# Token norms in quarters: sums by four column tiles, root and reciprocal on packed rows, spread by small products, and one pass for the norms of queries and keys

## The chip, the cores and the metric

The kernel runs on one core of a Trainium2 chip as one program. The metric is the device time of one execution, in microseconds, as a median over runs. Beside it stands a profile of one more execution.

## What is computed

Two transformer blocks of two layers each run on 512 tokens of width 1024; the first block also has 256 context tokens. All of it is float32. What bears on the change are the norms over the features of each token:

```python
def rmsnorm(x, g):
    y = x * lax.rsqrt(jnp.mean(x * x, axis=-1, keepdims=True) + RMS_EPS)
    return y * g
def modulate(x, g, shift, scale):
    return rmsnorm(x, g) * (1 + scale) + shift
def layer_norm(x, g, b):
    mu = jnp.mean(x, -1, keepdims=True)
    var = jnp.mean(jnp.square(x - mu), -1, keepdims=True)
    return (x - mu) * lax.rsqrt(var + LN_EPS) * g + b
```

- `modulate` stands before the mixer and before the mixture of experts in both layers of the first block: 768 tokens (256 context and 512 latent) three times, 512 tokens once. A last `rmsnorm` ends the block.
- In the first mixer `rmsnorm` is also taken of the query latent (384 features, 3 chunks of 128), of the key-value latent (256 features, 2 chunks), and of each head of 64 features in `gq` (8 heads, 4 chunks) and `gk` (2 heads, 1 chunk), for 768 tokens.
- `layer_norm` stands four times in the second block, for 512 tokens.
- The vectors for shift and scale come from `silu(c) @ w_ada`, a matrix of 2 x 1024 x 6144 that is read once.

## The kernel before

Activations lie with features on the 128 partitions (8 chunks of 128) and tokens along the free axis. The program is a row of stages. Each is a block with one instruction list for each engine, and all engines meet between two stages. Loads that a stage names as `ahead` or `beside` are issued by SyncE at that stage's start.

**A norm stage** (`norm_stage`) takes a list of jobs, one for each span of tokens (256 or 512). In a job ScalarE squares each chunk (L507). TensorE multiplies it with a matrix of ones, which leaves the sum over all features in all 128 rows for each token (L533). ScalarE takes the root (L511), VectorE the reciprocal (L547) and then one multiply for each chunk by gain and reciprocal (L552), and ScalarE adds the shift (L516). A layer norm (`center=True`) first sums the features themselves (L527) and subtracts the mean (L545). A float32 product shows as two matmul records. ScalarE loads another function table at the first root of a stage in which the table is not in place.

**Which stages there are:** `mod0` (2 jobs), `norm_qk`, `ffn0` (2), `mod1` (2), `ffn1` (1), `final` (1, no shift), and the layer norms `ln00`, `ln01`, `ln10`, `ln11` (1 each). `norm_qk` has 14 jobs: for either span of tokens one for the query latent, one for the key-value latent, one for each chunk of `gq`, one for `gk`; its root and total are held in two buffers each.

**The conditioning** (class `Conditioning`) is `w_ada` in 48 units of 1 MB, 8 units to a group, 6 groups. A unit is multiplied by `multiply` (L388): four matmuls with 32 columns of weights each, which write to four quarters of the partitions and read four different pieces of 512 columns. A finished group is copied by ScalarE (L395), turned by TensorE (L402) and added to the bias by VectorE (L410). This work goes beside other stages: a `Beside(ada, fetched, units, done)` says which units SyncE fetches in the stage, which units TensorE multiplies after which step, and which group is finished after which step. From unit 16 on five slots of memory go round, so unit u is fetched when unit u-5 has been multiplied. Units 8 to 15 are beside `mod0`, 16 to 29 beside `norm_qk`, 30 to 39 beside `ab_up`, 40 to 47 beside `rope`.

**The first mixer** is `ab_in` (projections), `norm_qk`, `ab_up` (38 products with the up-projections, copied out by ScalarE and VectorE in turn), `rope` (14 items; for each a matmul that swaps pairs (L917) and three VectorE operations; TensorE is at most two items ahead; then two small matmuls of `Distances`, their copies, and 8 copies by ScalarE (L948)), and attention.

## Time and profile before

| | us |
|---|---|
| median of 3 runs | 4196.33 (4196.19 to 4197.29) |
| profiled execution | 4192.28, its span 4190.4 |
| TensorE busy in the span | 3682.4 (88%) |
| VectorE busy | 2510.7 (60%) |
| ScalarE busy | 1570.1 (37%) |
| GpSimd busy | 194.9 (5%) |
| DMA, mean over the span | 161 GB/s |

The span runs from the first to the last instruction. The shares are means over stages with different limits: what a change in a stage is worth has to be read from that stage's own rows.

### The profile page before, as it was taken

To read this page: it belongs to the slowest core of one execution; us is meant where nothing else is said; L and a number is where in the kernel's file an instruction comes from. 1 tells how busy PE (TensorE), PEld (TensorE's weight loads), DVE (VectorE), ACT (ScalarE), POOL (GpSimd) and SP (SyncE) were. 2 spreads that over 40 slices of the span, in tenths; PEclk is the share of its full clock that TensorE was granted. 3 is DMA by queue.
4 is the path that set the end of the run, shared out by engine and by line. 5 is a ranking of instruction groups with operands and counts; after the bars stand their busy time and mean duration, and the time that the engine had idled before them with its cause. 6 is when DMAs were issued, how large, how long until landed. Compare 5 with 4: busy or idle time off the path is not lost. (4 is left out here: it accounts for less than half of the span.)

```text
span 4190.4 us, 51613 instructions
## 1 busy us (share of the span) xinstructions
PE 3682.4 (88%) x18221; PEld 2836.7 (68%) x18221; DVE 2510.7 (60%) x3105; ACT 1570.1 (37%) x2030; POOL 194.9 (5%) x306
## 2 busy tenths in 40 slices
PE   7988998599999589877799998698899979879997
PEld 4523766588888379555688886485687858557875
DVE  2044663588888442764688886545555566356654
ACT  2012652377777310462577786113111021111101
POOL 0000000111111100000111111000000000000000
PEclk9988998699999699998899999799999989989999
DMA  7064811699999220002899995421233246113321
GB/s 251 33 229 125 222 28 46 246 361 383 377 367 355 84 81 22 21 1 98 297 361 362 367 362 201 131 71 46 70 96 94 80 61 91 31 40 97 94 92 49
DMA packets 372842, 672.85 MB, mean 161 GB/s; under 512 B 48238, under 2 KB 246715, under 8 KB 366560
## 3 DMA queue, kind: packets, MB, share of 16 engines
q1 hardware_dynamic: 350477, 639.24, 45.6%
q0 software_dynamic: 21600, 31.51, 2.1%
q8 instruction: 89, 1.46, 0.1%
q14 instruction: 49, 0.40, 0.0%
q10 hardware_dynamic: 627, 0.24, 0.0%
HBM read 651.46 MB, written 66.58 MB: 171 GB/s over the span
## 5 line engine op out<-in xcount | busy, mean ns | idle before, releaser
L1844 DVE TENSOR_TENSOR moe0b_w_lo<-moe_raw,moe0b_w_hi 128x2048 fp32r<-128x2048 f32 x118 | 264.5, 2287 | 57.5 <-ACT moe0b_w_hi L1766 54.1
L1844 DVE TENSOR_TENSOR moe1b_w_lo<-moe_raw,moe1b_w_hi 128x2048 fp32r<-128x2048 f32 x112 | 251.1, 2288 | 55.0 <-ACT moe1b_w_hi L1766 51.8
L1766 ACT ACTIVATE moe0b_w_hi<-moe_raw 128x2048 fp32r<-128x2048 f32 x118 | 218.9, 1922 | 31.5 <-PEq L1373 31.5
L1766 ACT ACTIVATE moe1b_w_hi<-moe_raw 128x2048 fp32r<-128x2048 f32 x112 | 207.9, 1925 | 23.6 <-PEq L1373 23.6
L507 ACT ACTIVATE ln_squares<-all_x 128x512 f32<-128x512 f32 x32 | 19.2, 630 | 388.8 <-DVE all_x L545 388.8
L1700 PE MATMUL moe0b_gate_ps<-moe0b_w_hi,moe0b_feats_hi 128*128 128x512 f32 x264 | 110.7, 419 | 10.0 <-DVE moe0b_feats_lo L1850 5.9
L1700 PE MATMUL moe1b_gate_ps<-moe1b_w_hi,moe1b_feats_hi 128*128 128x512 f32 x256 | 107.2, 419 | 10.0 <-DVE moe1b_feats_lo L1850 5.9
L1844 DVE TENSOR_TENSOR moe0b_w_lo<-all_h,moe0b_w_hi 128x2048 fp32r<-128x2048 f32 x48 | 107.2, 2286 | 1.8 <-PE moe0b_up_ps L1700 1.8
L1844 DVE TENSOR_TENSOR moe1b_w_lo<-all_h,moe1b_w_hi 128x2048 fp32r<-128x2048 f32 x48 | 107.2, 2284 | 1.7 <-PE moe1b_up_ps L1700 1.7
L1700 PE MATMUL moe0b_up_ps<-moe0b_w_hi,moe0b_feats_hi 128*128 128x512 f32 x264 | 104.3, 395 | 0.0
L1700 PE MATMUL moe0b_gate_ps<-moe0b_w_lo,moe0b_feats_hi 128*128 128x512 f32 x264 | 104.3, 395 | 0.0
L1700 PE MATMUL moe0b_up_ps<-moe0b_w_lo,moe0b_feats_hi 128*128 128x512 f32 x264 | 104.2, 395 | 0.0
L1700 PE MATMUL moe0b_up_ps<-moe0b_w_hi,moe0b_feats_lo 128*128 128x512 f32 x264 | 103.9, 394 | 0.0
L1700 PE MATMUL moe0b_gate_ps<-moe0b_w_hi,moe0b_feats_lo 128*128 128x512 f32 x264 | 103.8, 393 | 0.0
L1700 PE MATMUL moe1b_up_ps<-moe1b_w_lo,moe1b_feats_hi 128*128 128x512 f32 x256 | 101.0, 394 | 0.0
L1700 PE MATMUL moe1b_up_ps<-moe1b_w_hi,moe1b_feats_hi 128*128 128x512 f32 x256 | 100.9, 394 | 0.0
L1700 PE MATMUL moe1b_gate_ps<-moe1b_w_lo,moe1b_feats_hi 128*128 128x512 f32 x256 | 100.8, 394 | 0.0
L1700 PE MATMUL moe1b_gate_ps<-moe1b_w_hi,moe1b_feats_lo 128*128 128x512 f32 x256 | 100.6, 393 | 0.0
L1700 PE MATMUL moe1b_up_ps<-moe1b_w_hi,moe1b_feats_lo 128*128 128x512 f32 x256 | 100.6, 393 | 0.0
L2834 ACT ACTIVATE ffn1u_mixed<-ffn1u_mixed 128x512 f32<-128x512 f32 x22 | 13.9, 632 | 214.9 <-DVE ffn1u_mixed L2794 214.9
L2834 ACT ACTIVATE ffn0u_mixed<-ffn0u_mixed 128x512 f32<-128x512 f32 x22 | 13.9, 632 | 214.9 <-DVE ffn0u_mixed L2794 214.9
L1109 DVE TENSOR_REDUCE attn_top<-attn_scores 128x1 f32<-128x768 f32 (+1 forms) x96 | 72.3, 776 | 36.8 <-PE attn_scores L1026 36.8
(640 smaller groups left out, 10442.8 us busy)
## 6 DMA issues: line engine op xcount, KB each, us to landing
moe_raw<-in_moe_w_gate SPq DMA_DIRECT2D x166, 512.0 KB, 5.8
moe_raw<-in_moe_w_up SPq DMA_DIRECT2D x166, 512.0 KB, 10.4
all_h<-in_moe_w_down SPq DMA_DIRECT2D x128, 512.0 KB, 8.0
moe_raw<-in_moe_w_down SPq DMA_DIRECT2D x128, 512.0 KB, 9.6
all_ahead<-in_ffn_w_up SPq DMA_DIRECT2D x88, 512.0 KB, 5.0
all_ahead<-in_moe_w_gate SPq DMA_DIRECT2D x62, 512.0 KB, 6.0
all_ahead<-in_moe_w_up SPq DMA_DIRECT2D x62, 512.0 KB, 11.0
y_rows<-all_zero SPq DMA_DIRECT2D x43, 512.0 KB, 6.7
```

The costliest lines, as they stand in the source:

```text
L507: nc.scalar.activation(squares[n % n_sq][:, c, 0:j.n], j.dst[c] if center else src, ACT.Square).then_inc(squared, 1)
L1109: V.tensor_reduce(top[:, s:s + 1], scores[s][:, 0:t.keys], AX.X, ALU.max, negate=True).then_inc(topped, 1)
L1700: last = nc.tensor.matmul(acc[:], x[:, c, :], w[:, m, j, :], start=c == 0 and step == 0, stop=c == DC - 1 and step == 2)
L1766: A_.activation(w_hi[r % HIGH][:], raw[slot][:], ACT.Copy).then_inc(rounded, 1)
L1844: V.tensor_tensor(w_lo[r % SPLIT][:], raw[r % RAW][:], w_hi[r % HIGH][:].bitcast(F32), ALU.subtract).then_inc(split, 1)
L2834: nc.scalar.activation(mixed[s][:], mixed[s][:], ACT.Silu).then_inc(silu_ready, 1)
```

## The change

- **Sums.** A chunk of n tokens is no longer summed by one matmul with 128 columns of ones over all n tokens, but by four with 32 columns each, every one over a quarter of the tokens (`QuadRows.add`). Quarter q lands in partitions 32q to 32q+31, so the total of 512 tokens has 128 columns in place of 512.
- **Root and reciprocal** are taken once for a stage, on these packed rows: 128 columns for 512 tokens, 192 for 768.
- **Spread.** Four small products with a constant matrix `pick` (64 rows each, two quarters of the tokens in either half of the rows) bring the reciprocals back to all partitions and all tokens (`QuadRows.spread`); VectorE reads them from PSUM. A layer norm does the same with the mean, which is scaled on packed rows first.
- **Squares.** Where nothing is centred, VectorE squares chunks 1, 4 and 7 and ScalarE the other five. With two jobs all squares come first, then one root and one reciprocal, then all scaling. The work beside a stage comes at its end.
- **`norm_qk`** becomes `latent_norm_stage`: 10 parts of 768 tokens, squared by ScalarE and VectorE in turn through a ring of three buffers, all sums in one PSUM tile (seven kinds of sum, each in its own row of a quarter), one root, one reciprocal, then seven spreads through two buffers. It loads two constants first (`norm_sums`, 112 KB, and `norm_pick`, 896 KB), on which the first sum waits.
- **Units** of the conditioning: 2 beside `norm_qk` (16 and 17, at its end), 19 beside `ab_up` (18 to 36), 11 beside `rope` (37 to 47). Groups 2 and 3 are finished in `ab_up`, 4 and 5 in `rope`.
- The constant `half_ones` (64 KB) gives way to `pick` (128 KB) in the first stage, and `rope` puts the table `by_bucket` into memory of `wkv`.

```diff
+    sums, pick = np.zeros((PART, NORM_KINDS, QUAD), np.float32), np.zeros((PART, NORM_KINDS, 2, PART), np.float32)
+    for q in range(QUADS):
+        for c in range(NORM_CQ):
+            for half in range(2):
+                rows = slice(half * HEAD, (half + 1) * HEAD)
+                sums[rows, c, 2 * c + half], pick[q * QUAD + 2 * c + half, c, q % 2, rows] = 1.0 / HEAD, 1.0
+        for kind, size in ((NORM_CQ, Q_LORA), (NORM_CKV, KV_LORA)):
+            sums[:, kind, NORM_CQ + kind], pick[q * QUAD + NORM_CQ + kind, kind, q % 2, :] = 1.0 / size, 1.0
+    k["norm_sums"], k["norm_pick"] = sums, pick
...
+class QuadRows:
+
+
+
+
+    def __init__(self, nc, n):
+        self.nc, self.m = nc, n // QUADS
+
+    def add(self, out, columns, x, start, stop):
+        for q in range(QUADS):
+            last = self.nc.tensor.matmul(out[q * QUAD:(q + 1) * QUAD, :], columns, x[:, q * self.m:(q + 1) * self.m], start=start, stop=stop)
+        return last
+
+    def spread(self, out, pick, rows, into):
+        for h in range(2):
+            group = slice(h * PAIR, (h + 1) * PAIR)
+            for i in range(2):
+                last = self.nc.tensor.matmul(out[:, h, i * self.m:(i + 1) * self.m], pick[group, i, :], rows[group, :], start=True, stop=True)
+            last.then_inc(into, 1)
+
+
+def halves(x):
+    return x.rearrange("p (h m) -> p h m", h=2)
+
...
+            act.wait_ge(summed, 1)
+            nc.scalar.activation(root[:], total[:, 0:n_tok // QUADS], ACT.Sqrt, scale=inv_n, bias=P.eps[:, eps:eps + 1]).then_inc(rooted, 1)
+            for n, j in enumerate(jobs):
                 if j.bias is not None:
...
+            if center:
+                for n, j in enumerate(jobs):
+                    for c, src in enumerate(j.src):
+                        last = quads[n].add(mean[:, cols[n]], P.ones[:, 0:QUAD], src, c == 0, c == C - 1)
+                last.then_inc(mean_ready, 1)
+                pe.wait_ge(mean_taken, 1)
+                for n in steps:
+                    quads[n].spread(mean_by_half[n], P.pick, mean_rows[:, cols[n]], mean_out)
...
+                    last = quads[n].add(total[:, cols[n]], P.ones[:, 0:QUAD], squares[n][:, c, :], c == 0, c == C - 1)
+            last.then_inc(summed, 1)
+            pe.wait_ge(inverted, 1)
+            for n in steps:
+                quads[n].spread(by_half[n], P.pick, root[:, cols[n]], root_spread)
+            if beside is not None:
+                for n in steps:
                     beside.tensor(pe, n)
...
+            V = nc.vector
+            if center:
+                dve.wait_ge(mean_ready, 1)
+                V.tensor_scalar(mean_rows[:], mean[:, 0:n_tok // QUADS], -inv_n, None, ALU.mult).then_inc(mean_taken, 1)
+                dve.wait_ge(mean_out, 2 * len(jobs))
+                for n, j in enumerate(jobs):
+                    for c, src in enumerate(j.src):
+                        V.tensor_tensor(halves(j.dst[c]), halves(src), mean_by_half[n], ALU.add).then_inc(centered, 1)
...
+                    if on_dve[c]:
+                        V.tensor_tensor(squares[n][:, c, :], src, src, ALU.mult).then_inc(by_dve, 1)
+            dve.wait_ge(rooted, 1)
+            V.reciprocal(root[:], root[:]).then_inc(inverted, 1)
+            if center:
+                dve.wait_ge(by_act, n_act * len(jobs))
+            dve.wait_ge(root_spread, 2 * len(jobs))
+            for n, j in enumerate(jobs):
+                for c, src in enumerate(j.src):
+                    V.scalar_tensor_tensor(halves(j.dst[c]), halves(j.dst[c] if center else src), j.gain[c], by_half[n],
+                                           ALU.mult, ALU.mult).then_inc(scaled, 1)
+            if beside is not None:
+                for n in steps:
                     beside.vector(dve, n)
...
+def latent_norm_stage(nc, P, K, tag, parts, eps, ahead, beside):
...
+        def _(sp):
+            sp.dma_start(sums[:], K["norm_sums"]).then_inc(consts_in, 16)
+            sp.dma_start(pick[:], K["norm_pick"]).then_inc(consts_in, 16)
+            ahead.start(sp)
+            beside.sync(sp)
+
+        @block.scalar
+        def _(act):
+            for n in range(0, len(parts), 2):
+                if n >= RING:
+                    act.wait_ge(added, n - RING + 1)
+                nc.scalar.activation(squares[n % RING][:], parts[n][1], ACT.Square).then_inc(by_act, 1)
+            act.wait_ge(added, len(parts))
+            nc.scalar.activation(root[:], total[:, 0:m], ACT.Sqrt, bias=P.eps[:, eps:eps + 1]).then_inc(rooted, 1)
+            for n in range(len(order)):
+                beside.scalar(act, n)
+
+        @block.tensor
+        def _(pe):
+            pe.wait_ge(consts_in, 32)
+            for n, (kind, _, _) in enumerate(parts):
+                pe.wait_ge(by_dve if n % 2 else by_act, n // 2 + 1)
+                quads.add(total[:, 0:m], sums[:, kind, :], squares[n % RING], n == 0, n == len(parts) - 1).then_inc(added, 1)
+            pe.wait_ge(inverted, 1)
+            for n, kind in enumerate(order):
+                if n >= 2:
+                    pe.wait_ge(scaled, ends[n - 2] + 1)
+                quads.spread(spread[n % 2], pick[:, kind], root, spread_ready)
+                beside.tensor(pe, n)
+
+        @block.vector
+        def _(dve):
+            V = nc.vector
+            for n in range(1, len(parts), 2):
+                if n >= RING:
+                    dve.wait_ge(added, n - RING + 1)
+                V.tensor_tensor(squares[n % RING][:], parts[n][1], parts[n][1], ALU.mult).then_inc(by_dve, 1)
+            dve.wait_ge(rooted, 1)
+            V.reciprocal(root[:], root[:]).then_inc(inverted, 1)
+            dve.wait_ge(added, len(parts))
+            for n, kind in enumerate(order):
+                dve.wait_ge(spread_ready, 2 * (n + 1))
+                for _, x, gain in [part for part in parts if part[0] == kind]:
+                    V.scalar_tensor_tensor(halves(x), halves(x), gain, spread[n % 2][:, :, 0:2 * m], ALU.mult, ALU.mult).then_inc(scaled, 1)
+                beside.vector(dve, n)
...
-                       beside=Beside(ada, range(16, 35), {n: (16 + n,) for n in range(14)}, {10: (2,)}))
+            parts = [(NORM_CQ, cq[:, c, :], col("mla_q_norm")(c)) for c in range(QC)]
+            parts += [(NORM_CKV, ckv[:, c, :], col("mla_kv_norm")(c)) for c in range(KVC)]
+            parts += [(c, gq[:, c, :], P.gq_gain[:]) for c in range(H_B // 2)]
+            parts += [(NORM_GK, gk[:], col("gqa_k_norm")(0))]
+            latent_norm_stage(nc, P, K, "norm_qk", parts, 0, up_weights,
+                              Beside(ada, range(16, 21), {6: (16, 17)}, {}))
...
-                              beside=Beside(ada, range(35, 40), {3 * n + 1: (30 + n,) for n in range(10)}, {12: (3,), 32: (4,)}))
-
+                              beside=Beside(ada, range(21, 42), {2 * n: (18 + n,) for n in range(19)}, {12: (2,), 28: (3,)}))
+
+            distances.by_bucket = wkv[0:T5_BUCKETS + 1].rearrange("p c n -> p (c n)")[:, 0:distances.SPAN]
...
-                       Beside(ada, range(40, 48), {n + 4: (40 + n,) for n in range(8)}, {13: (5,)}), distances)
+                       Beside(ada, range(42, 48), {n + 3: (37 + n,) for n in range(11)}, {6: (4,), 13: (5,)}), distances)
```

## Rows read from the trace of the kernel before

**Rows 1.** Windows by stage: `mod0`, `norm_qk`, `ab_up`, `rope`, `ffn0`, `mod1`, `ffn1`, `final`, `ln00`.
```profile
core 0: us, PE busy (x) PEld busy (x) DVE busy (x) ACT busy (x) POOL busy (x), PEclk, DMA share, GB/s
37.40:72.10 34.70, 23.24 (x101) 10.62 (x101) 13.94 (x19) 18.28 (x36) 0.00 (x0) 0.80 0.75 302
199.50:262.10 62.60, 35.86 (x157) 10.08 (x157) 46.77 (x36) 16.95 (x35) 0.00 (x0) 0.82 0.91 354
262.10:342.80 80.70, 77.55 (x272) 31.18 (x272) 13.58 (x22) 8.81 (x21) 0.00 (x0) 0.97 0.19 65
342.80:387.30 44.50, 29.40 (x100) 6.64 (x100) 27.80 (x44) 7.29 (x11) 0.00 (x0) 0.76 0.59 217
684.60:715.50 30.90, 13.13 (x32) 6.79 (x32) 13.75 (x18) 17.82 (x35) 0.00 (x0) 0.75 0.00 0
1444.60:1477.60 33.00, 15.20 (x32) 8.59 (x32) 13.75 (x19) 17.84 (x36) 0.00 (x0) 0.71 0.20 64
1946.00:1964.40 18.40, 7.14 (x17) 3.00 (x17) 8.74 (x9) 11.57 (x18) 0.00 (x0) 0.78 0.00 0
2647.60:2667.40 19.80, 9.24 (x16) 3.75 (x16) 8.74 (x9) 6.25 (x11) 0.00 (x0) 0.76 0.33 106
2969.60:2995.80 26.20, 14.21 (x32) 5.85 (x32) 13.62 (x17) 12.14 (x18) 0.00 (x0) 0.90 0.31 80
```

**Rows 2.** Timeline of `ffn0`: start, us, engine, line, operation, shapes, count, idle before.
```profile
684.62 2.56 ACT L507 ACTIVATE ffn_squares<-all_x 128x256 f32<-128x256 f32 x8 [73.44 <-PEq L603]
687.20 1.28 ACT L511 ACT_TABLE_LOAD   x1
688.85 0.47 ACT L511 ACTIVATE ffn_root<-ffn_total,all_eps 128x256 f32<-128x256 f32 x1 [0.37 <-PE ffn_total L533]
689.36 1.75 DVE L547 RECIPROCAL ffn_root<-ffn_root 128x256 f32<-128x256 f32 x1 [5.03 <-ACT ffn_root L511]
691.14 3.26 DVE L552 SCALAR_TENSOR_TENSOR all_h<-all_x,all_scale,ffn_root 128x256 f32<-128x256 f32 x8
694.87 4.25 ACT L507 ACTIVATE ffn_squares<-all_x 128x512 f32<-128x512 f32 x8
695.54 9.41 PE L533 MATMUL ffn_total<-ffn_squares,all_ones 128*128 128x512 f32 x16 [6.72 <-ACT ffn_squares L507]
704.98 0.69 ACT L511 ACTIVATE ffn_root<-ffn_total,all_eps 128x512 f32<-128x512 f32 x1 [5.86 <-PE ffn_total L533]
705.70 3.35 DVE L547 RECIPROCAL ffn_root<-ffn_root 128x512 f32<-128x512 f32 x1 [11.30 <-ACT ffn_root L511]
709.09 5.39 DVE L552 SCALAR_TENSOR_TENSOR all_h<-all_x,all_scale,ffn_root 128x512 f32<-128x512 f32 x8
709.88 5.36 ACT L516 ACTIVATE all_h<-all_h,all_mod 128x512 f32<-128x512 f32 x8 [4.21 <-DVE all_h L552]
```

**Rows 3.** Timeline of `ln00`: the sum for the mean, and the centring.
```profile
2969.57 7.11 PE L527 MATMUL ln_mean<-all_x,all_ones 128*128 128x512 f32 x16 [1.05 <-PEq L603]
2976.72 4.87 DVE L545 SCALAR_TENSOR_TENSOR all_x<-ln_mean,all_x 128x512 f32<-128x512 f32 x8 [7.46 <-PE ln_mean L527]
```

**Rows 4.** Timeline of TensorE beside `mod0`: eight units of the conditioning.
```profile
59.54 7.16 PE L388 MATMUL early_ada_acc<-early_ring,all_cond 128*32 128x512 f32 x64
```

**Rows 5.** Groups by shape, TensorE: busy us, mean ns of one, idle before.
```profile
L1050 PE MATMUL attn_n_mixed<-attn_n_probs_t,all_h 128*64 128x128 f32 x768 | 48.8, 277 | 0.0
L1026 PE MATMUL attn_n_scores<-na_k,na_q 64*128 64x256 f32 x128 | 20.4, 377 | 0.0
```

**Rows 6.** Timeline of weight loads in `mod0`: the last unit there.
```profile
65.63 0.16 PEld L388 LDWEIGHTS early_ada_acc<-early_ring,all_cond 128*32 128x32 f32 x8 [0.78 <-DMA early_ring<-in_w_ada]
```

**Rows 7.** DMA issues in `norm_qk`: KB each, median us to landing.
```profile
ab_up_wq<-in_mla_w_q_up SPq DMA_DIRECT2D x1, 1152.0 KB, 6.0
```

**Rows 8.** Timeline of `ab_up`: one unit of the conditioning between two products.
```profile
303.90 1.06 PE L388 MATMUL ab_up_ada_acc<-all_ahead,all_cond 128*32 128x512 f32 x8
```

**Rows 9.** Timeline of ScalarE at the end of `rope`.
```profile
380.74 5.96 ACT L948 ACTIVATE l_ka<-low_kr 32x768 f32<-32x768 f32 x8 [0.39 <-DVE l_gk L934]
```

More of the change, by code:

```diff
@@ L488, in norm_stage @@
         block = ctx.enter_context(nc.Block())
-        first = np.cumsum([0] + [len(j.src) for j in jobs]).tolist()
+        steps = range(len(jobs))
+        on_dve = [not center and c % 3 == 1 for c in range(C)]
+        n_act, n_dve = on_dve.count(False), on_dve.count(True)
+        inv_n = jobs[0].inv_n
         if ahead is not None or beside is not None:
@@ new lines, in _ @@
+            if beside is not None:
+                for n in steps:
+                    beside.vector(dve, n)
+def latent_norm_stage(nc, P, K, tag, parts, eps, ahead, beside):
+    n_tok, RING = TOK, 3
+    m = n_tok // QUADS
+    with ExitStack() as ctx:
+        sb, ps, sem = scope(nc, ctx, tag)
+        quads = QuadRows(nc, n_tok)
+        sums, pick = sb("sums", [PART, NORM_KINDS, QUAD]), sb("pick", [PART, NORM_KINDS, 2, PART])
+        squares = [sb(f"squares{n}", [PART, n_tok]) for n in range(RING)]
+        root = sb("root", [PART, m])
+        total = ps("total", [PART, BANK])
+        spread = [ps(f"spread{n}", [PART, 2, BANK]) for n in range(2)]
+        consts_in, by_act, by_dve, added = sem("consts_in"), sem("by_act"), sem("by_dve"), sem("added")
+        rooted, inverted, spread_ready, scaled = sem("rooted"), sem("inverted"), sem("spread_ready"), sem("scaled")
+        block = ctx.enter_context(nc.Block())
+        order = [kind for n, (kind, _, _) in enumerate(parts) if n == 0 or parts[n - 1][0] != kind]
+        ends = [max(n for n, part in enumerate(parts) if part[0] == kind) for kind in order]
+        @block.sync
+        def _(sp):
[40 more added lines that the diff above has]
+                beside.vector(dve, n)
@@ L569, in modulate_jobs @@
         bias=[P.mod[:, l, 3 * which * DC + c, w:w + 1] for c in range(DC)],
-        sums=P.ones, size=D,
+        size=D,
     ) for t, w in spans]
@@ L2172, in lat_norm_job @@
                             gain=[gain(c) for c in range(DC)], bias=None if bias is None else [bias(c) for c in range(DC)],
[L2173 removed]
+                    size=D)]
 def final_norm(nc, P, ahead):
```

108 lines of the change are left out of this document (41 added, 67 removed).

## The prediction

> **What bounds the kernel now.** I went first to the windows by stage, since the change touches ten stages of very different kinds and their busy shares can't be averaged [rows 1]. The reader is to see that a norm stage is no engine's stage: in `ffn1` 18.4 us hold 7.1 of TensorE, 8.7 of VectorE and 11.6 of ScalarE, one behind the other. `ab_up` is different: TensorE is busy for 77.6 of 80.7 us, so whatever is added to its list there comes on top. `norm_qk` has the DMA engines at 0.91 for 62.6 us at 354 GB/s: its 14 jobs run beside a stream of units, and the two hold each other up.
>
> The timeline of `ffn0` shows the chain inside a norm [rows 2]: squares, sum (its last record ends 5.9 us after the last square), root, reciprocal, scaling with the shift one chunk behind, and then the same again for the second job. Only the first root has a table load before it (1.28), which begins when the squares end (684.62 + 2.56) and lies under the sum. A layer norm has a sum of 7.1 and a centring of 4.87 ahead of that [rows 3].
>
> **The prices.** *Adding a chunk.* 16 records over 512 columns take 7.11, so 0.444 each, and 128 columns would be 0.111 [rows 3]. Do four column tiles run side by side? The 64 records of eight units take 7.16, that is 0.112 each for 512 columns: yes, four at a time [rows 4]. A quarter of that is 0.028 for 128 columns and 0.22 for the 8 records of a chunk. That is the lower bound. The nearest row in size has 128 columns and two tiles side by side: 48.8/768 = 0.0635, which is 0.008 over the half of 0.111 [rows 5]. If the 0.008 is what a record costs besides its columns, a chunk takes 8 x 0.036 = 0.3, which I use. If 0.0635 is a floor for any record, it takes 0.51, the upper bound. With no overlap at all it would be 0.89.
>
> *A spread.* 8 records with full-width weights and 64 rows. Such records of 256 columns take 20.4/128 = 0.159 where one after the other would be 0.222, thus 0.64 to 0.89 for 512 tokens [rows 3, 5]; with the hand-over I take 0.95, and 1.8 at half clock. For two jobs I take 1.6 (1.3 of columns and a second start).
>
> *Packed rows.* The root falls from 0.69 to 0.47 as 512 columns become 256, so 0.37 for 128 and 0.42 for 192; the reciprocal from 3.35 to 1.75, so 0.95 and 1.35 [rows 2]. Scaling is unchanged at 0.41 for 256 columns and 0.67 for 512, with the last shift 0.76 behind [rows 2]. Reading the factor from PSUM is bounded by the centring, which reads PSUM and takes 0.61 a chunk: a possible gain of 0.5 a stage [rows 3].
>
> *The table load.* It costs nothing now because the sum covers it. With the sum gone quickly it stands bare: 1.28 after ScalarE's last square. So the shorter sum doesn't end the wait; the table load is late next.
>
> **Stage by stage.** `ffn0`: ScalarE does five of eight squares, 1.60 + 2.66 = 4.26, and VectorE's three are done sooner; table 1.28; root 0.42; reciprocal 1.35; spread 1.6; scaling 3.26 + 5.39; last shift 0.76; hand-overs and the change of stage 0.6. That is 18.9 where the window has 30.9: 12.0 less [rows 1, 2]. `mod1` works at a lower clock (0.71 in its window), so I add 1.3 to the spread and 0.6 to the sums: 20.8 for 33.0, 12.2 less.
>
> `ffn1`: 2.66 + 1.28 + 0.37 + 0.95 + 0.95 + 5.39 + 0.76 and 0.5 of hand-overs = 12.9 for 18.4: 5.5 less. `final` has no shift, but the lower clock: 2.66 + 1.28 + 0.4 + 0.37 + 0.95 + 1.8 + 5.39 + 0.6 = 13.5 for 19.8: 6.3 less.
>
> `ln00`: mean 8 x 0.3 and a start, 2.5; scaling it on 128 columns 0.3; spread 0.95; centring 4.87, with the squares following; last square 0.6; table 1.28; root 0.37; reciprocal 0.95; spread 0.95; scaling 5.39; shift 0.76; hand-overs 0.7. That is 19.6 for 26.2: 6.6 less, and 26.4 for four, the other three taken alike.
>
> `mod0`: the last unit's data holds its end. TensorE waits for it until 65.63 [rows 6], and the loads before it don't change. After it came the unit, the wait for ScalarE's shifts, copy, turn and bias up to 72.1 [rows 1]. All norm work is now done some 9 us before 65.6 (37.4 + 18.9 = 56.3), so only the wait goes: 2.7 less, not 12.
>
> `norm_qk`: the first sum waits for 1008 KB of constants. SyncE issues them first; the nearest load of that size, 1152 KB, landed 6.0 us after its issue [rows 7], so 205.5. Behind them the weights and the units come 2.5 us later, which hides: only units 16 and 17 are wanted, and at the end. Ten chunks of 768 tokens: 8 x 0.05 = 0.4 at full clock and 0.73 at half; TensorE has idled for 6 us, so 0.6 each, to 211.5. Root, reciprocal and hand-overs 1.9; first spread 1.4, to 214.9. VectorE scales ten parts of 768 columns in 0.94 each; the five kinds with one part are held by spreads of 1.4, 2 us more, so 226.3; the two units end at 227.6. About 28.5 us for 62.6: 34.1 less, with 25.5 (everything at full clock and overlapped) to 35 (spreads at half clock) as bounds.
>
> What it hands on: `ab_up` gets nine more units of 1.06 [rows 8] into an engine that has no room: 9.5 more. Their data is in time (5 MB a loop of ten products, 20 us or more). `rope` gets units 37 to 39, about 0.8 more; group 4's copy and turn between items (0.53 as a 512-column ScalarE operation, 0.44 for four records of 128 columns, and hand-overs) 1.5; unit 41's load in front of its tables, up to 2.5 us of a queue, 1.5; and at the end unit 47 now stands behind the last but one item, so that copy, turn, the `Distances` products (1.1) and their copies come before ScalarE's eight copies, which now start right behind VectorE's last operation [rows 9]: 3.0. Together 6.8. The three stages: 34.1 - 9.5 - 6.8 = 17.8 less.
>
> **The sum.** 12.0 + 12.2 + 5.5 + 6.3 + 26.4 + 2.7 + 17.8 = 82.9. The profiled execution took 4192.28, so 4109.4; the median of the runs is 4.05 above it, so 4113.4. The 64 KB more in the first stage are 0.2 us at 354 GB/s.
>
> **One rule against it.** Records of 128 columns were seen at 0.0635 with two tiles side by side, and nothing in the profile shows four tiles at that size [rows 5]. The Trainium skill (TensorE: Matmul & The Clock Gate, section "Wait — 56ns, not 53.3ns?") says that the engine's sequencer can spend about 62 ns on each matmul, which binds once the array's work for it is shorter. By that rule a chunk takes 0.50, and packing into quarters stops paying at that point; the row is consistent with it as well as with my reading.
>
> **The rivals.**
> - *Each record has a floor of 0.0635.* A chunk costs 0.51. The mean takes 1.7 more in each layer norm (6.7), the sums of `ffn0` and `mod1` 16 x 0.51 = 8.2 and now outlast squares and table load by 2.9 each (5.8). For it: the row is exactly there. Against: half of 0.111 explains most of it. Time: 4126.
> - *The first mixer gives nothing back.* The conditioning work is the same, and `ab_up` has no idle TensorE; if constants, half clock and the longer `rope` take 17.8 together, 4131. For it: the DMA share of 0.91 in `norm_qk`, so the old stage was also useful transfer time [rows 1]. Against: 65 GB/s in `ab_up` leaves room.
> - *The quarters run one after the other.* 0.89 a chunk at full clock: 23 more in the layer norms, 7.6 in the single norms, 11.5 in `ffn0` and `mod1`, 7.4 in `norm_qk`: 4163. Against it stand the 64 records [rows 4].
> - *Slower: one after the other and at half clock,* since TensorE works little in these stages. At 1.78 a chunk the layer norms lose 80, the single norms 22, the double ones 33, `norm_qk` 21, against my sum: 4268. It passes no gain at about 1.2 us a chunk.
> - *No gain in all* would need just that 1.2: 4196.
>
> **How the numbers follow.** My case 0.70, the floor 0.17, the mixer 0.07, serial at full clock 0.03, slower 0.02, no gain 0.01. The predicted time is my case's. Below: sums at 0.22 (2.5), spreads at 0.64 (3.5), the mixer's lower bounds (6), factors from PSUM (4), so 4097. Above: 0.51 a chunk (12.5), all spreads at half clock (9), the mixer's upper bounds (9.5), so 4144. The range 4096 to 4145 holds the floor and the mixer too; about 2 in 10 lies outside. About 0.2%, 8 us, is what a measurement of this kernel can tell from no change: faster 0.97, same 0.01, slower 0.02.
>
> **What would show it.** Adding a chunk: TensorE's records in the layer norms' mean, 64 records in 2.4 us (1.8 or 4.1 by the bounds, 7 or more if serial). The table load bare between the last square and the root, with no TensorE work above it. Reciprocals of 0.95 and 1.35. `norm_qk` about 28 us with TensorE idle for the first 6. `ab_up` near 90, `rope` near 51 with ScalarE's eight copies 3 us behind VectorE's last addition. `mod0` shorter by less than 4. I am wrong if TensorE's clock stays low in the layer norms (spreads of 1.8), if the ring in `norm_qk` starves, or if the next stages begin slower because TensorE has idled more before them.

## The result and the profile after

The changed kernel takes 4099.08 us (median of 4 runs, 4098.90 to 4101.79) where the kernel before takes 4196.81: ratio 0.9768, 95% interval [0.9751, 0.9785], 97.7 us less. Predicted were 4113.4 and a range of 4096 to 4145. The profiled execution took 4101.79; it is compared below with the profiled 4192.28 of before, a difference of 90.5 both in time and in span.

The windows by stage of the changed kernel, in the order of [rows 1] with the first attention between `rope` and `ffn0` (from each stage's first operation to the next stage's):

```profile
core 0: us, PE busy (x) PEld busy (x) DVE busy (x) ACT busy (x) POOL busy (x), PEclk, DMA share, GB/s
38.80:71.90 33.10, 20.88 (x212) 7.85 (x213) 12.94 (x24) 15.15 (x29) 0.00 (x0) 0.65 0.79 318
199.06:225.00 25.94, 15.12 (x153) 8.92 (x153) 15.70 (x16) 4.53 (x6) 0.00 (x0) 0.80 0.84 329
225.00:311.54 86.54, 85.54 (x344) 30.95 (x344) 13.77 (x23) 8.81 (x21) 0.00 (x0) 1.00 0.72 249
311.54:357.84 46.30, 31.99 (x128) 7.07 (x128) 28.25 (x45) 7.90 (x13) 0.00 (x0) 0.78 0.46 176
357.84:582.90 225.06, 209.25 (x1664) 151.23 (x1664) 138.14 (x293) 141.09 (x324) 0.00 (x0) 0.96 0.51 122
660.20:678.50 18.30, 6.34 (x144) 5.14 (x145) 12.74 (x23) 14.56 (x28) 0.00 (x0) 0.64 0.00 1
1407.30:1425.80 18.50, 6.49 (x144) 5.67 (x144) 12.75 (x24) 14.60 (x29) 0.00 (x0) 0.59 0.36 114
1895.30:1908.40 13.10, 4.38 (x72) 2.63 (x72) 8.20 (x12) 9.69 (x15) 0.00 (x0) 0.58 0.01 2
2592.30:2606.10 13.80, 4.37 (x72) 3.49 (x72) 9.74 (x17) 5.90 (x10) 0.00 (x0) 0.62 0.50 159
2908.19:2927.40 19.21, 8.22 (x144) 4.58 (x144) 11.48 (x18) 11.80 (x18) 0.00 (x0) 0.67 0.42 110
```

`norm_qk` fell from 62.6 to 25.9. `ab_up`, whose TensorE now works 85.5 of 86.5 us, grew by 5.8, `rope` by 1.8. Such a change can be booked by the shift of each stage's first operation between the two traces. Summed up, in us saved against what was forecast:

| part | forecast | by the starts |
|---|---|---|
| `mod0` | 2.7 | 0.2 |
| first mixer to the start of its attention | 17.8 | 29.3 |
| that attention and `ab_out` | 0 | -5.1 |
| `ffn0`, `mod1` | 12.0, 12.2 | 12.6, 14.5 |
| `ffn1`, `final` | 5.5, 6.3 | 5.3, 7.5 |
| `ln00`, `ln01`, the other two together | 6.6, 6.6, 13.2 | 7.0, 8.0, 15.0 |
| drifts of the stages between | 0 | -3.8 |
| sum | 82.9 | 90.5 |

A second trace of the changed kernel (under `changed_again` below) gives the norm stages the same to 0.5 us, but only 26.0 for the mixer and 84.0 in all. The norms' column is firm, then, and the mixer's good to some 3 us.

The timeline of `ffn0` after, the answer to [rows 2]:

```profile
660.19 4.24 ACT L556 ACTIVATE ffn_squares<-all_x 128x256 f32<-128x256 f32 x10 [73.23 <-PEq L729]
660.21 2.90 DVE L606 TENSOR_TENSOR ffn_squares<-all_x 128x256 f32<-128x256 f32 x6 [0.32 <-PEq L729]
660.65 5.08 PE L498 MATMUL ffn_total<-ffn_squares,all_ones 128*32 128x64 f32 x128 [1.56 <-ACT ffn_squares L556]
664.45 1.28 ACT L558 ACT_TABLE_LOAD   x1
665.81 0.42 ACT L558 ACTIVATE ffn_root<-ffn_total,all_eps 128x192 f32<-128x192 f32 x1
666.26 1.35 DVE L608 RECIPROCAL ffn_root<-ffn_root 128x192 f32<-128x192 f32 x1 [3.15 <-ACT ffn_root L558]
667.67 1.26 PE L505 MATMUL ffn_spread<-ffn_root,all_pick 64*128 64x64 f32 x16 [1.94 <-DVE ffn_root L608]
668.98 8.49 DVE L614 SCALAR_TENSOR_TENSOR all_h<-all_x,all_scale,ffn_spread 128x256 f32<-128x256 f32 x16 [1.36 <-PE ffn_spread L505]
669.49 8.73 ACT L563 ACTIVATE all_h<-all_h,all_mod 128x256 f32<-128x256 f32 x16 [3.26 <-DVE all_h L614]
```

One chain where there were two, with squares of 4.24, a root of 0.42, a reciprocal of 1.35 and a scaling of 8.49 (forecast: 4.26, 0.42, 1.35 and 8.65). One detail will matter: the sum's last record ends at 660.65 + 5.08 = 665.73, the very moment at which the table load ends.

The mean in `ln00`, the answer to [rows 3]:

```profile
2908.19 1.95 PE L498 MATMUL ln_mean<-all_x,all_ones 128*32 128x128 f32 x64 [1.05 <-PEq L729]
2910.20 0.29 DVE L598 TENSOR_SCALAR ln_mean_rows<-ln_mean 128x128 f32<-128x128 f32 x1 [2.33 <-PE ln_mean L498]
2910.55 0.72 PE L505 MATMUL ln_mean_spread<-ln_mean_rows,all_pick 64*128 64x128 f32 x8 [0.41 <-DVE ln_mean_rows L598]
2911.35 4.87 DVE L602 TENSOR_TENSOR all_x<-all_x,ln_mean_spread 128x512 f32<-128x512 f32 x8 [0.86 <-PE ln_mean_spread L505]
```

64 records in 1.95 are 0.030 each: four column tiles side by side, with 0.24 for a chunk where 0.30 was taken, near the lower bound of 0.22. The records' starts show how: four follow each other 0.006 to 0.007 us apart, and the next four begin 0.109 us after the first of them.

No run below separates the shorter sums from the packed root and reciprocal; only the rows do. In `ln00` the mean's sum is 5.2 shorter and its scaling and spread take back 1.2, and the root went from 0.69 to 0.37 and the reciprocal from 3.35 [rows 2] to 0.95, for which the second spread takes back 1.4.

### The profile page after: what moved, and what is told of

Read it like the earlier page. It is cut to its first block and busy times, and to the rows that moved or that the text cites. A ratio compares the mean times of both kernels' runs of the same rounds, so it can differ in the third digit from the quotient of the medians.

```text
span 4099.9 us, 53555 instructions
## 1 busy us (share of the span) xinstructions
PE 3623.2 (88%) x19213; PEld 2822.3 (69%) x19213; DVE 2468.4 (60%) x3112; ACT 1543.6 (38%) x1975; POOL 194.2 (5%) x306
```

## The experiments

Each was timed beside the kernel before, whose median lay between 4196.4 and 4198.2 throughout; four groups of runs used four chips. The experiments' own runs spread over 5 to 20 us, the longest mostly at a lower mean granted clock. Effects of a few microseconds are therefore read from the traces, by the shifts of the stages' starts. These have a spread too. Between the two traces of the changed kernel, with no edit at all, the starts drift apart by 1.6 us up to `norm_qk`, 3.6 up to the attention and 6.5 up to the end. `norm_qk` took 25.9 in one and 27.0 in the other, `ab_in` 127.2 and 128.5. So a shift counts only where it arises in the stage that was edited and is larger than that stage's own spread.

### The norms alone, and the mixer alone

```diff
 norms_only: nine stages by the new norm_stage
-latent_norm_stage(nc, P, K, "norm_qk", parts, 0, up_weights, Beside(ada, range(16, 21), {6: (16, 17)}, {}))
+old_norm_stage(nc, P, "norm_qk", norm_jobs(...), 0, ahead=up_weights,
+               beside=Beside(ada, range(16, 35), {n: (16 + n,) for n in range(14)}, {10: (2,)}))
 ab_up and rope: the units of before
 mixer_only: the reverse; the nine stages by old_norm_stage
```

> The nine other norm stages as changed, but the stage norm_qk, its two neighbours' share of the conditioning units and the rope's order as before. My theory, by the shift of starts between the two traces: the nine norm stages took 12.6, 14.5, 5.3, 7.5, 7.1, 8.0 and some 15 for the last two, about 70 us, and the first mixer 29, so the time goes back up by some 29 to about 4128. Rival 1 (the mixer gives everything back; the 5.2 us that attention takes longer in the trace of the changed kernel are caused by it): the mixer is worth only 24 and the time is about 4122. Rival 2 (most of the gain is the mixer's, by overlap with other stages that the starts don't show): above 4140.

> The stage norm_qk and the units as changed, all other norm stages as before. My theory: the gain is the mixer's alone, 29 us of 4196.8, so 4168, and with the run of the norms alone the two gains add up to the whole 98 within 2 us. Rival (the slower starts of ab_up, rope and attention eat the shorter norm_qk): 4190 or more. If the gains of both runs add up to much less than 98, the parts help each other, which the stage windows don't show.

Norms alone also loads the constant `half_ones` again, which the old `norm_qk` reads. Measured: 4124.3 (4121.2 to 4130.0, ratio 0.9826 [0.9813, 0.9839]) and 4170.3 (4167.6 to 4175.9, ratio 0.9934 [0.9920, 0.9948]), with 4196.95 before. The norms are worth 72.7 and the mixer 26.7, together 99.3 for the 97.7 of the whole: the parts add up. In the trace of the norms alone, the attention starts 26.9 us later than in the changed kernel's, but `ab_out` only 21.7 later. The attention took 219.9 us there and 225.1 in the changed kernel. So the 5 us there belong to the changed mixer, as the first rival said. The price itself lies between that rival's 24 and the theory's 29: 26.7 with the mixer alone, 25.0 as the whole less the norms.

### All squares on ScalarE

```diff
-        on_dve = [not center and c % 3 == 1 for c in range(C)]
+        on_dve = [False] * C
```

> As changed, but ScalarE makes all squares of the stages without a mean (VectorE made three of eight). It undoes the split and leaves the packing. My theory: ScalarE's squares precede the table load and the root, so ffn0 and mod1 lose 6 squares there (0.37 and 0.53 each, 2.6 us a stage), ffn1 and final 3 (1.6 each), mod0 nothing, as it waits for its units: 8.4 us more, 4107.5. Rival (the sum hides them, so the split is worth nothing): 4099, with the table load then still bare behind the last square.

Measured: 4110.2 (4105.9 to 4115.0, ratio 0.9788 [0.9774, 0.9801]). By the starts `ffn0` lost 2.4, `mod1` 3.1, `ffn1` 1.6 and `final` 1.2: 8.3 where 8.4 was expected, so VectorE's three squares of eight are 8 of the 98 us, and the rival (nothing) falls. The rest of the longer span lies in stages that the edit doesn't touch.

### The root's table ahead of the squares

```diff
-        on_dve = [not center and c % 3 == 1 for c in range(C)]
+        warm = sb("warm", [PART, 1])
+        on_dve = [not center and c % 2 == 1 for c in range(C)]
...
         def _(act):
+            nc.scalar.activation(warm[:], P.eps[:, eps:eps + 1], ACT.Sqrt).then_inc(warmed, 1)
```

> As changed, with a root of one element as ScalarE's first instruction of each norm stage, and four of eight squares on VectorE instead of three. The table load of 1.28 us then comes before the squares instead of between the last square and the root; in a layer norm it lies under the mean. My theory (the load stands bare in each stage): 1.28 less in each of four layer norms, and in the others as much as the squares' new split allows, 1.2 each in ffn0 and mod1 (1.28 + 8 squares of 0.37 to 0.53 beside VectorE's 0.97 a pair) and 0.5 each in ffn1 and final: 8.5 in all, 4090.6. Rival 1 (the sums end after the load anyway, so the load hides): 4099. Rival 2 (a Square needs another table than the root, so each stage then loads twice): 5 to 10 slower, with two table loads in each stage.

Measured: 4099.9 (4096.4 to 4105.2, ratio 0.9768 [0.9755, 0.9782]). In all nothing was gained, as rival 1 said; the theory fell. The timeline of `ffn1`, first of the changed kernel and then of this one:

```profile
1895.98 3.16 PE L498 MATMUL ffn_total<-ffn_squares,all_ones 128*32 128x128 f32 x64 [1.77 <-ACT ffn_squares L556]
1898.03 1.28 ACT L558 ACT_TABLE_LOAD   x1
1899.32 0.37 ACT L558 ACTIVATE ffn_root<-ffn_total,all_eps 128x128 f32<-128x128 f32 x1
```

```profile
1893.44 1.28 ACT L551 ACT_TABLE_LOAD   x1 [45.21 <-PEq L731]
1893.48 2.50 DVE L608 TENSOR_TENSOR ffn_squares<-all_x 128x512 f32<-128x512 f32 x4 [0.32 <-PEq L731]
1895.51 3.59 PE L498 MATMUL ffn_total<-ffn_squares,all_ones 128*32 128x128 f32 x64 [3.14 <-ACT ffn_squares L558]
1899.15 0.37 ACT L560 ACTIVATE ffn_root<-ffn_total,all_eps 128x128 f32<-128x128 f32 x1 [2.13 <-PE ffn_total L498]
```

In the changed kernel the sum ends at 1899.14 and the table load at 1899.31. They run side by side, so taking the load away can win 0.2 there. In the edited kernel the load delays ScalarE's first square, and TensorE, which takes the chunks in order, starts 2.1 us into the stage instead of 0.7 and stands until then: the root begins 5.7 us after the stage's start where it began 4.0 after. A TensorE that takes VectorE's chunks first was not tried, so the edit shows what this order costs and not what the load alone is worth. Only the layer norms, where the load hides under the mean, gained: from the start of the mean to the root 9.48 instead of 10.01 in `ln00`, half a microsecond, and between 0.5 and 1.0 in the other three, where 1.28 was expected. Now the root of `ln00` waits 0.78 for the sum.

### The mean, one column tile after the other

```diff
-                    for c, src in enumerate(j.src):
-                        last = quads[n].add(mean[:, cols[n]], P.ones[:, 0:QUAD], src, c == 0, c == C - 1)
+                    for q in range(QUADS):
+                        for c, src in enumerate(j.src):
+                            last = nc.tensor.matmul(mean[q * QUAD:(q + 1) * QUAD, cols[n]], P.ones[:, 0:QUAD],
+                                                    src[:, q * m:(q + 1) * m], start=c == 0, stop=c == C - 1)
```

> As changed, but the records of the mean in the four layer norms come in another order: the 16 of one column tile together, then the next tile's, instead of one for each of the four tiles in turn. Same records, same columns, same sums. My theory: the 0.030 us that a record of 128 columns takes are four tiles working side by side, and neighbours in the queue must be for different tiles, so now a record takes 0.111 (a quarter of 0.444), the mean 7.1 instead of 1.95, and four layer norms 20.6 more: 4119.6. Rival (the engine works on quarters in any order, or a record is bound by its issue and not by its columns): 1.95 again and 4099.

Measured: 4113.9 (4106.0 to 4122.0, ratio 0.9797 [0.9783, 0.9810]). The mean of `ln00` in that kernel's timeline, and its first 12 records alone:

```profile
2909.98 5.93 PE L575 MATMUL ln_mean<-all_x,all_ones 128*32 128x128 f32 x64 [1.04 <-PEq L732]
2915.94 0.29 DVE L601 TENSOR_SCALAR ln_mean_rows<-ln_mean 128x128 f32<-128x128 f32 x1 [6.29 <-PE ln_mean L575]
2909.98 1.47 PE L575 MATMUL ln_mean<-all_x,all_ones 128*32 128x128 f32 x12 [1.04 <-PEq L732]
```

The same 64 records take 5.93 instead of 1.95, at the full granted clock in both: 0.093 each on average where I expected 0.111. Within one tile the price was right: the 12 records take 1.47, of which the last one's own length is 0.27, so they start 0.109 apart. What is missing to 0.111 arises at the three changes of tile: around each some eight records stand in pairs, 0.005 to 0.030 apart, as records of two tiles side by side would. By the stages' lengths the four layer norms are 16.7 longer (3.4 to 4.6 each; 20.6 expected). So the tiles work side by side when neighbours in the queue are for different tiles, and the mechanism, not the number of records, makes the gain.

### Where `mod0`'s gain went

```diff
             def _(sp):
-                if ahead is not None:
-                    ahead.start(sp)
                 if beside is not None:
                     beside.sync(sp)
+                if ahead is not None:
+                    ahead.start(sp)
```

> As changed, but in mod0 the eight conditioning units are fetched before the 2 MB of ab_in's first weights. My theory (the stage mod0 is held by the last unit's data, 67.7 us in the trace, so nothing of the norm's gain shows): the units land 5 to 6 us sooner and mod0 ends some 3 us sooner, then at its next bound, ab_in's weights, which land at about 67.7 instead: 4096. Rival (ab_in waits for all the later data anyway, so what mod0 gains ab_in loses): ab_in ends as before, 4099.

Measured: 4096.8 (4095.0 to 4106.9, ratio 0.9769 [0.9756, 0.9783]). The timeline of TensorE's weight loads at the end of `mod0`, of the changed kernel and then of this one:

```profile
67.72 0.16 PEld L403 LDWEIGHTS early_ada_acc<-early_ring,all_cond 128*32 128x32 f32 x8 [2.31 <-DMA early_ring<-in_w_ada]
71.88 0.29 PEld L928 LDWEIGHTS ab_in_bank<-all_h,all_ahead 128*128 128x128 f32 x1 [0.92 <-issue]
```

```profile
61.62 0.20 PEld L403 LDWEIGHTS early_ada_acc<-early_ring,all_cond 128*32 128x32 f32 x8 [2.34 <-DMA early_ring<-in_w_ada]
66.91 1.35 PEld L928 LDWEIGHTS ab_in_bank<-all_h,all_ahead 128*128 128x128 f32 x4 [2.32 <-DMA all_ahead<-in_ab_w_in]
```

The last unit comes 6.1 us sooner, `ab_in` starts 5.0 sooner and also ends 4.9 sooner, so the rival falls; now its weights hold it. Of the 5.0, 0.8 was there at `mod0`'s start, and 4.2 are the stage's (28.9 instead of 33.1), more than the 3 expected: the DMA engines' share in `mod0` rose from 0.79 to 0.92.

### ScalarE's copies first in `rope`

```diff
             def _(act):
+                act.wait_ge(rotated, 1)
+                for src, dst in spread:
+                    nc.scalar.activation(dst, src, ACT.Copy).then_inc(copied, 1)
...
-                act.wait_ge(rotated, len(items))
-                for src, dst in spread:
-                    nc.scalar.activation(dst, src, ACT.Copy).then_inc(copied, 1)
```

> As changed, but in the stage rope ScalarE makes its eight copies of the shared key first, as soon as the first item is turned, and the conditioning's rows and the distances after them. My theory (the end of rope is ScalarE's serial list: turn's copy, distances, then 5.95 us of copies that start 2.8 us behind VectorE's last addition): the copies hide under VectorE's work, rope ends with the distances' copies at about 352.5 instead of 357.8, and the time is 5 less: 4094. Rival (the attention behind it is held by something else, its weights or its code, and gives the 5 back): rope is 5 shorter and the time 4099.

Measured: 4091.0 (4082.2 to 4093.7, ratio 0.9739 [0.9726, 0.9753]). In the changed kernel ScalarE's end of `rope`, the answer to [rows 9], was

```profile
350.84 0.74 ACT L2338 ACTIVATE l_distance_rows<-rope_distance_acc 8x512 f32<-8x512 f32 x2 [1.70 <-PE rope_distance_acc L2333]
351.61 5.95 ACT L1074 ACTIVATE l_ka<-low_kr 32x768 f32<-32x768 f32 x8
```

and VectorE's last addition ends at 348.86, so the copies start 2.8 behind it, as forecast. With the copies first, the attention starts 7.9 us sooner, 5.5 of them `rope`'s (2.4 stood there before it began), where `rope` took 39.7 to 41.2 in the nine traces without an edit there and 34.1 here; 1.1 is given back in the attention, whose stall (below) it doesn't touch.

### A constant in two parts in `norm_qk`

```diff
-            pe.wait_ge(consts_in, 32)
+            pe.wait_ge(sums_in, 16)
...
+            pe.wait_ge(pick_in, 16)
             pe.wait_ge(inverted, 1)
```

> As changed, but in norm_qk the adding records wait for the 112 KB of norm_sums alone, and only the first spread waits for the 896 KB of norm_pick. My theory (TensorE idles for the first 5 us for a constant that it needs 8 us later): the adds start some 3 us sooner, at about 202 instead of 205, norm_qk is 3 shorter, 4096. Rival (the adds are paced by the squares and by TensorE at half clock after its idle time, so an earlier start only spreads them out): within 1 us of 4099.

Measured: 4098.5 (4092.4 to 4101.3, ratio 0.9759 [0.9746, 0.9772]). The adds, in the changed kernel and then in this one:

```profile
204.08 4.35 PE L498 MATMUL norm_qk_total<-norm_qk_squares,norm_qk_sums 128*32 128x192 f32 x56 [5.65 <-DMA norm_qk_pick<-const_norm_pick]
208.62 1.44 PE L498 MATMUL norm_qk_total<-norm_qk_squares,norm_qk_sums 128*32 128x192 f32 x24 [0.19 <-DVE norm_qk_squares L677]
```

```profile
201.96 5.92 PE L498 MATMUL norm_qk_total<-norm_qk_squares,norm_qk_sums 128*32 128x192 f32 x80 [3.46 <-DMA norm_qk_sums<-const_norm_sums]
```

The start is 2.1 sooner, the end 2.2, and the stage 0.9. But the changed kernel's 25.9 is the shortest `norm_qk` of the ten traces in which that stage is as changed; the others have 26.3 to 27.5, and the two with this edit 25.0 and 25.1. The gain is thus 0.9 to 2.5, and the truth lies between theory and rival.

### Three units moved back to `ab_up`

```diff
-  ab_up: {2 * n: (18 + n,) for n in range(19)}, {12: (2,), 28: (3,)}
-  rope:  {n + 3: (37 + n,) for n in range(11)}, {6: (4,), 13: (5,)}
+  ab_up: {**{2 * n: (18 + n,) for n in range(16)}, **{32 + n: (34 + n,) for n in range(6)}}, {12: (2,), 28: (3,)}
+  rope:  {n + 3: (40 + n,) for n in range(8)}, {3: (4,), 10: (5,)}
```

> As changed, but the three units 37 to 39 are multiplied in ab_up instead of rope, and rope's other units and turns stand three items earlier. My theory (ab_up's end moved by 5.8 us for nine more units while TensorE has no idle time there, so a unit costs its 1.06 wherever it stands in that list, and in rope it costs little because TensorE idles between items): ab_up 3.2 longer; rope 1 to 2 shorter, because its last turn and the distances no longer stand behind VectorE's last item: within 2 of 4100. Rival (a unit in ab_up costs only what 5.8/9 = 0.64 says, as the data of TensorE's list overlaps): ab_up 1.9 longer, and the time 4099 or less.

Measured: 4100.8 (4100.1 to 4104.7, ratio 0.9773 [0.9760, 0.9787]). `ab_up` grew by 2.8 up to `rope`'s first issue and by 3.4 in TensorE's busy time (0.9 to 1.1 a unit), `rope` shrank by 1.7. A unit costs about its 1.06 in `ab_up`; the rival's 0.64 is refuted.

### The attention that became longer

The waits of TensorE in the changed kernel, from 352 to 420 us (in all, times, longest), and TensorE's timeline there:

```profile
PE attn_mixed L1176 <- issue: 2.6, 1, 2.6
```

```profile
392.40 0.87 PE L1176 MATMUL attn_mixed<-attn_probs_t,l_va 128*64 128x128 f32 x10
395.86 1.97 PE L1176 MATMUL attn_mixed<-attn_probs_t,l_va 128*64 128x128 f32 x14 [2.59 <-issue]
```

TensorE stands 2.59 us between two records of one group, with no wait for anybody, and comes back at the lower granted clock, 0.50 of the full one, thus 1.2 GHz (two windows, of the changed kernel and then of the kernel with the late store):

```profile
396.00:402.00 6.00, 6.00 (x20) 3.62 (x21) 0.96 (x1) 0.60 (x1) 0.00 (x0) 0.50 0.47 51
```

```profile
396.00:402.00 6.00, 5.02 (x27) 3.16 (x26) 4.21 (x8) 2.36 (x5) 0.00 (x0) 1.00 0.00 0
```

A stop of 2.5 to 4.4 us, ended between 389 and 399, was in all ten traces with the new mixer and the early store, and in neither trace with the old mixer. In each of the ten TensorE restarts 2.2 to 2.5 us after a transfer of instructions (DMA queue 8) is on record: in the changed kernel it stops at 393.3, the transfer stands at 393.4 and the restart at 395.9; with the mixer alone these are 392.9, 395.0 and 397.3, with all squares on ScalarE 396.0, 396.3 and 398.5. The store of the distances' rows runs beside them (2560 KB, a DMA share of 0.47 at 50 GB/s for some 45 us).

```diff
                 if store is not None:
+                    sp.wait_ge(normed, N // 2)
                     store.store(sp)
```

> As changed, but in the first attention SyncE issues the 2.5 MB store of the distances' rows only when a quarter of the turns is done, instead of 4 us after the start. In every trace with the new norm_qk, and in none with the old one, TensorE stands 2.5 to 4.4 us some 38 us after the start of the attention, with no wait that the profile shows, while an instruction transfer runs beside this store, and works at half clock after it; the attention is 5 us longer. My theory (the transfer of TensorE's next instructions is held up by the store's packets): no such stall at its place, the attention 5 us shorter, 4094. Rival 1 (the stall is where TensorE outruns its instruction transfer, whatever else the DMA engines do): it stays, 4099. Rival 2 (the store meets a later instruction transfer instead): the stall moves to some 15 us or more behind the store's new start.

Measured: 4101.0 (4086.3 to 4106.4, ratio 0.9769 [0.9752, 0.9785]). The medians don't show a gain, but the trace shows the stop gone, nowhere in the attention is there another, and the attention takes 219.6 us. So both rivals fall. Its lengths in the traces: 219.9 before, 219.9 with the norms alone, 225.1 changed, 224.9 with the mixer alone, 226.2 with the copies first, 219.6 with the late store. From its first operation to `ab_out`'s it takes 221.4 to 224.2 in the ten traces with the stop and 216.7 to 217.9 in the four without. So stall and low clock are the 5 us, and the store takes part in them.

The DMA queues also show which transfer is late. Here are those between 17 and 35 us after the attention's start, in the changed kernel (375 to 393.2) and then with the late store (375 to 392):

```profile
q1 hardware_dynamic: 358, 0.92, 47.3%
```

```profile
q8 instruction: 1, 0.02, 0.3%
q14 instruction: 2, 0.02, 0.3%
```

With the late store a queue-8 transfer comes 22.1 us after the attention's start and the next at 35.0 (21.1 and 34.7 in `together`). With the early store none comes before 35.5 to 36.8 in any of the ten. That fits the theory that the store's packets hold the transfer up until TensorE has nothing left to run; that queue 8 feeds TensorE is a reading of the times. With the norms alone the store is issued at the same distance, 3.8 us, from the attention's start, and transfers come at 17.1 and 32.5 without a stop; why it does so badly only behind the new mixer is not shown.

### The changed kernel again, and everything together

```diff
 together: units_first + copies_first + pick_late + store_late, and
+            if center:
+                nc.scalar.activation(warm[:], P.eps[:, eps:eps + 1], ACT.Sqrt).then_inc(warmed, 1)
```

> The changed kernel itself, without any edit, on the chip of these runs. Its own runs lay between 4098.9 and 4101.8; the kernels of the experiments spread over 5 to 20 us each. If that spread is the experiments', this run stays within 3 us of 4099; if it is the day's and the chip's, this one spreads over 5 to 20 us too, and shifts of less than some 5 us are to be read from the traces' stages and not from the medians. Its trace should show the stall of 2.5 to 3 us in the first attention again.

> As changed, with five edits at once: the units first in mod0, the copies first in rope, the adds of norm_qk waiting for norm_sums alone, the store of the distances' rows after a quarter of the attention, and the root of one element ahead of the squares in the layer norms alone (not in the other norms, where the sums' end was found right behind the table load). My theory, by the shifts of starts in the single runs' traces: 5.0 + 5.5 + 1 + 5.5 + 4 times 0.5 = 19 less than the changed kernel, some 4080. Rival (they share their gains: an earlier start only waits at the next load): each stage's gain shows but the stages behind give some back, 4087 or more. Against it: the single runs' shifts stayed in place to the end of the trace.

Measured: the changed kernel itself 4095.3 (4087.8 to 4108.3, ratio 0.9757 [0.9743, 0.9770]), with mean clocks of 0.935 in its shortest run and 0.930 in its longest, and the stall again (2.51 us at 400.38). The spread of the runs is thus not the experiments'. Together 4077.5 (4072.4 to 4084.4, ratio 0.9716 [0.9702, 0.9729]): all its runs are below all of the changed kernel, 17.8 less by the medians where 19 was expected. The rival (4087 or more) falls. By the starts it gains 4.2 before `ab_in`, 5.6 more by the start of the attention, 6.4 in the attention, 0.5 in `ln00` and 0.8 in `ln10`, against the changed kernel's first trace. The 24.2 at the end hold more than these 17.5: 5.5 arise between the first block's `ffn0` and `mod1`, in a stage that no edit touches, and are spread.

## Why the prediction was right, and where not

*The mechanism* was right where most of the gain lies: packed sums, roots and reciprocals near the forecast prices, `norm_qk` a stage of 26 us, `ab_up` paying for its units. It failed in three places told below: the bare table load, `mod0`, and the attention. The time lies 14.3 below the forecast. Of that 7.6 lie between the sum and the profiled execution (4101.8 where 4109.4 was summed up). The other 6.8 are the step from profile to median, which I took as 4.05 upward as before, and which is 2.7 downward for the changed kernel. The second profile of the same kernel took 4108.3, so neither part is clear of spread.

That the sum comes so near is partly luck. The norms outside `mod0` and the mixer saved 7.5 more than forecast and the mixer 11.5 more, while `mod0` fell short by 2.5, the attention took 5.1 and the drifts 3.8.

*The mixer, the largest miss.* The terms for `ab_up` (9.5) and `rope` (6.8) were mis-sized: 5.8 and 1.8. For `ab_up`, TensorE's busy time grew by 8.0 and its idle time fell by 2.1 [rows 1]. I had counted nine units at full price and overlooked the clock at the stage's start. The windows of its first 8 us, before and after:

```profile
262.10:270.00 7.90, 7.90 (x23) 3.64 (x24) 0.69 (x1) 0.38 (x1) 0.00 (x0) 0.71 0.01 2
```

```profile
225.00:233.00 8.00, 8.00 (x36) 3.32 (x37) 0.69 (x1) 0.76 (x2) 0.00 (x0) 1.00 0.90 344
```

TensorE arrives at the full clock now, where the granted clock was 0.71, and 7.9 times 0.29 is 2.3 us of work. The units' own price was right, as the three moved ones show. For `rope`, the delayed tables (1.5) cost nothing, since they landed sooner (6.7 us instead of 7.6 after its start), and group 4's turn cost 0.2 instead of 1.5; the 3.0 at its end were right (2.8), and `copies_first` won more than them. `norm_qk` saved 36.7 in this trace (35.1 to 36.3 in the nine others of the same stage) instead of 34.1: the constants were there at 204.1 instead of 205.5, and the spreads held VectorE less than the 2 us assumed.

*The attention*, costed at nothing, lost 5.1 by the stall. The step "what it hands on" ended at `rope`, one stage too soon.

*The prices.* A chunk 0.24 (0.30 taken): right by `tile_by_tile` for the reason given. Below the full clock it is more: in `ffn1` the last groups of four records start 0.21 apart instead of 0.109, so 0.43 a chunk. A spread 0.72 at full clock and 1.23 below it (0.95 and 1.8 taken). In `mod1` I had added 1.9 for the low clock, and its spreads took 1.21 for both jobs: most of the 2.3 missed there. A gain from factors in PSUM wasn't seen: 5.36 for 5.39.

*"The table load stands bare"* was half wrong. It precedes the root, but the sum ends with it, at the same moment in `ffn0` and 0.2 before in `ffn1`, and in `mod1` and `final` the root waits 0.28 and 0.38 for the sum:

```profile
1411.57 1.28 ACT L558 ACT_TABLE_LOAD   x1
1413.14 0.42 ACT L558 ACTIVATE mod_root<-mod_total,all_eps 128x192 f32<-128x192 f32 x1 [0.28 <-PE mod_total L498]
...
2595.01 1.28 ACT L558 ACT_TABLE_LOAD   x1
2596.67 0.37 ACT L558 ACTIVATE final_root<-final_total,all_eps 128x128 f32<-128x128 f32 x1 [0.38 <-PE final_total L498]
```

The terms were right because both arms of the fork are equally long; as a reason it failed, and the experiment built on it gained nothing in those stages. Only in the layer norms does the load stand bare, by 0.5 to 1.0.

*`mod0`* gained 0.2 in all instead of 2.7: the step "after it came the unit, copy, turn and bias" is right, and from the last data to `ab_in` it now takes 4.2 instead of 6.5. But of the wait's 3.1 us the last unit takes back 0.7, since it meets TensorE at the lower clock (1.76 instead of 1.06; window clock 0.65 instead of 0.80). The data itself ends at 67.7 instead of 65.6: 0.7 later in the stage, and 1.4 because the stage began later. That 1.4 can't be put down to the change: `mod0` starts between 37.5 and 38.8 in the thirteen traces with edits or the change, whatever the edit. The stage alone is 1.6 shorter.

*The rivals.* The floor of 0.0635 is refuted by 0.030, the serial one by the same row and by `tile_by_tile`, the mixer that gives all back by `mixer_only` (26.7 kept), and the last two, slower and no gain, by the time. A record of half the size settles the floor: `ffn0`'s first 16 records over 64 columns, at the full granted clock, show as

```profile
660.65 0.43 PE L498 MATMUL ffn_total<-ffn_squares,all_ones 128*32 128x64 f32 x16 [1.56 <-ACT ffn_squares L556]
```

with 0.22 for the last one's own length, and groups of four start 0.056 apart once they run, so 0.014 a record. The Trainium skill (TensorE: Matmul & The Clock Gate, section "Wait — 56ns, not 53.3ns?") gives some 62 ns of the sequencer for each matmul with hardware decode off. That doesn't bind here. The 0.030 alone wouldn't show it, since two records are one matmul and 32 matmuls in 1.95 are 0.061 each; the records over 64 columns do, at 0.028 a matmul. The same page of the Trainium skill, section "Measured speedup vs the span model", has tiles overlap with about 4 ns between them. As an estimate by that figure, four records of 0.111 would take some 0.12, thus 0.031 each. The trace's 0.030 is near it, with 0.006 to 0.007 between the starts of neighbours.

## What to carry to other kernels

Split a reduction over the columns into column tiles, and send neighbours in the queue to different tiles: the same 64 records took 1.95 us in turn and 5.93 tile by tile. Before removing a wait that stands at the end of a fork (here the table load), look when the other arm ends; where both end together only shortening both pays. Follow a change one stage further than its last edit: behind the new mixer TensorE met a store and a late instruction transfer and lost 5 us there. A change of order alone (units before weights, copies before the tail, a constant's wait and a store later, with the table load earlier in the layer norms) then gave another 18 us. And before reading a shift of a few microseconds from two traces, compare two traces of the same kernel.

## What the hardware showed unexpectedly

TensorE stopped for 2.5 to 4.4 us with no wait in the profile, restarted 2.2 to 2.5 us after a transfer of instructions that ran beside a 2560 KB store, and then worked some 6 us at 1.2 GHz; with the store moved, the transfer came some 14 us sooner and there was no stop. Records for one column tile start 0.109 us apart over 128 columns, and records for four tiles in turn 0.027 on average (0.014 over 64 columns). And the runs of one kernel on one chip spread over 20 us (4087.8 to 4108.3), the shortest at a mean granted clock of 0.935 and the longest at 0.930, where the first four runs of the same kernel lay within 3.
